# Latent attention with its value products in three reduced-precision passes, and new orders around it

## The reference

```python
h = layer_norm(x) * (1 + sc1) + sh1
proj = h @ w_in[l]                                   # q_c, kv_c, k_r, retention q, k, v, gate
a = mla_mixer(q_c, kv_c, k_r, ...)                   # latent attention, 8 heads
r = retention_mixer(r_q, r_k, r_v, r_g, ...)
y = jnp.concatenate([a, r], axis=-1) @ w_out[l]      # then layer norm, feed-forward, layer norm
# inside mla_mixer, for each head (q, k of 64 plain + 32 rotary columns; v of 64 columns)
sc = q_blk @ k.T * scale                             # masked to the causal half
p = softmax(sc)
out = p @ v
```

## Time and profile before

| | us |
|---|---|
| median of 3 runs | 2687.31 (2684.17 to 2688.14) |
| profiled execution: device time | 2691.6 |
| its span, first to last instruction | 2689.8 |
| PE busy | 2504.4 (93%) |
| DVE, POOL, ACT busy | 1350.4, 733.9, 651.6 |
| mean granted clock of TensorE | 0.963 of full speed |

### The profile page before, as it was taken

How to read it: one execution, slowest core, us unless ns; L and a number is a source line. 1 busy time by engine, 2 the same in 40 slices (tenths; PEclk the granted TensorE clock), 3 DMA queues, 4 the chain that set the end, 5 groups by cost and what they waited for, 6 DMA issues and landing times.

```text
span 2689.8 us, 29003 instructions
## 1 busy us (share of the span) xinstructions
PE 2504.4 (93%) x11544; PEld 1955.2 (73%) x11544; DVE 1350.4 (50%) x1513; ACT 651.6 (24%) x946; POOL 733.9 (27%) x490
## 2 busy tenths in 40 slices
PE   5998779989999999999998689999998999999998
PEld 3776556657678888888886368886586778888877
DVE  7556743434643444444435779996528321314433
ACT  3002224431432001101123421113204200025521
POOL 1241320015463332332345211210045223330011
PEclk9999879999999999999999899999999999979999
DMA  6651000022132332332222121112232521110021
GB/s 225 198 164 61 20 18 8 8 95 86 58 107 83 94 98 75 94 98 87 79 85 79 39 94 41 35 39 102 69 123 82 163 74 47 47 40 1 1 86 71
DMA packets 228851, 206.96 MB, mean 77 GB/s; under 512 B 15248, under 2 KB 203280, under 8 KB 227712
## 3 DMA queue, kind: packets, MB, share of 16 engines
q1 hardware_dynamic: 223552, 178.61, 21.9%
q10 hardware_dynamic: 3840, 21.89, 2.1%
q0 software_dynamic: 1344, 4.91, 0.5%
HBM read 180.35 MB, written 17.83 MB: 74 GB/s over the span
## 4 chain that ended last, share of the span: by engine, by line
PE 78%; DVE 9%; ACT 4%; issue 4%; PEld 2%; POOL 1%; DMA 1%; PEldq 1%; ACTq 0%; DVEq 0%; SPq 0%; POOLq 0%
PE G L1633 28%; PE G L304 25%; PE G L1099 2%; PE M L3001 2%; PE M L307 2%; PE G L2506 1%; PE M L400 1%; PE M L1649 1%; PE G L2322 1%; PE M L2322 1%; PE M L2986 1%; PE M L1010 1%; DVE WMAX L3024 1%; PE G L2349 1%; PE M L2508 1%
## 5 line engine op out<-in xcount | busy, mean ns | idle before, releaser
L278 POOL TENSOR_SCALAR WH<-RAW 128x1024 fp32r<-128x1024 f32 (+1 forms) x154 | 134.2, 872 | 887.2 <-PE G L1633 515.5
L304 PE MATMUL G<-HH,WH 128*128 128x512 f32 x1056 | 336.8, 400 | 14.5 <-POOL WL L2164 7.8
L304 PE MATMUL G<-HH,WL 128*128 128x512 f32 x1056 | 332.5, 396 | 0.0
L304 PE MATMUL G<-HL,WH 128*128 128x512 f32 x1056 | 332.4, 396 | 0.0
L281 POOL TENSOR_TENSOR WL<-RAW,WH 128x1024 fp32r<-128x1024 f32 (+1 forms) x154 | 299.4, 1944 | 12.9
L1633 PE MATMUL G<-HH,WH 128*128 128x512 f32 x640 | 227.2, 404 | 13.3 <-POOL WL L281 8.5
L304 PEld LDWEIGHTS G<-HH,WH 128*128 128x128 f32 x1056 | 188.2, 189 | 61.4 <-issue 19.2
L1633 PE MATMUL G<-HH,WL 128*128 128x512 f32 x640 | 223.8, 398 | 0.0
L1633 PE MATMUL G<-HL,WH 128*128 128x512 f32 x640 | 223.7, 398 | 0.0
L304 PEld LDWEIGHTS G<-HL,WH 128*128 128x128 f32 x1056 | 188.7, 188 | 42.2
L304 PEld LDWEIGHTS G<-HH,WL 128*128 128x128 f32 x1056 | 188.5, 188 | 42.1
(11 more groups left out here) (536 smaller groups left out, 4445.2 us busy)
## 6 DMA issues: line engine op xcount, KB each, us to landing
RAW<-in_w_ff SPq DMA_DIRECT2D x40, 512.0 KB, 3.8
RAW<-in_w_ff SPq DMA_DIRECT2D x80, 256.0 KB, 2.8
WVEC<-in_w_ada SPq DMA_DIRECT2D x24, 512.0 KB, 4.6
FVEC<-in_e_w_mod SPq DMA_DIRECT2D x24, 512.0 KB, 3.8
FVEC<-in_o_w_mod SPq DMA_DIRECT2D x24, 512.0 KB, 3.6
RAW<-in_o_w_in SPq DMA_DIRECT2D x24, 512.0 KB, 3.6
RAW<-in_e_w_in SPq DMA_DIRECT2D x20, 512.0 KB, 3.6
ADA<-in_w_ada SPq DMA_DIRECT2D x4, 2048.0 KB, 19.5
```

Source lines behind the costliest of these rows:

```text
L278: pool.tensor_scalar(hi, raw, 1.0, 0.0, ALU.mult, ALU.add).then_inc(w_high, 1)
L304: m = pe.matmul(G[s][:, n * w:(n + 1) * w], part[s][:, k, :], acts[i][:, k, n * w:(n + 1) * w], start=first, stop=last)
```

## The change

- The value product is split in three float32r passes. ACT still writes the exponentials PF (now three buffers). GpSimd copies them to PH (float32r, two buffers), DVE subtracts to get PL (three buffers), and the values have a high and a low part too (VPH, VPL). `values` now runs two steps behind the loop in place of one.
- In the DVE loop the new subtraction `p_low(g)` stands ahead of `smax(h + 1, i)`.
- The products for the first pair's queries and keys become a lead of mla. The second rotary part moves from head 0 to head 1; `q_part` and `k_part` move to steps 3 and 6, `ROW_AT` to (9, 11) for even heads, `v_part(0)` ahead of the maxima.
- The end of ret is run one head ahead on both engines. The first split of win waits until DVE's chains are done. The wf lead does tiles 4 to 7 of units 0 and 1, then the last `spread`, then tiles 0 to 3 of both; POOL passes the gate ahead of unit 2. In ein POOL makes the high parts of the first four units and not two. In odd three loads change places.

```diff
+        PF, PL = [[at(f"{n}{i}", [P, 512], t, (24 + 2 * i) * kb) for i in range(3)] for n, t in (("PF", F32), ("PL", F32R))]
+        PH = [Z(f"PH{i}", [P, 512], F32R, 12 + 2 * i) for i in range(2)]
...
 # PE, values(g)
-                pe.wait_ge(S("ml_e2"), g + 1)
-                pe.matmul(G[1][:, cols_], VP[:, kb_, first:first + P], PF[g % 4][:, 0:n], start=(kb_ == 0),
-                          stop=(kb_ == 4 * c + 3)).then_inc(S("ml_pv"), 1)
+                pe.wait_ge(S("ml_plo"), g + 1)
+                pe.matmul(G[1][:, cols_], vh, PH[g % 2][:, 0:n], start=(kb_ == 0), stop=False)
+                pe.matmul(G[1][:, cols_], vl, PH[g % 2][:, 0:n], start=False, stop=False)
+                pe.matmul(G[1][:, cols_], vh, PL[g % 3][:, 0:n], start=False, stop=(kb_ == 4 * c + 3))\
+                  .then_inc(S("ml_pv"), 1)
 # PE, the loop
-                if g:
-                    values(g - 1)
+                if g > 1:
+                    values(g - 2)
 # ACT, the exponential of step g
-                need(act, S("ml_pv"), g - 3)
+                need(act, S("ml_pv"), g - 2)
 # DVE
+            def p_low(g):
+                dve.wait_ge(S("ml_ph"), g + 1)
+                dve.tensor_tensor(PL[g % 3][:, 0:n], PF[g % 3][:, 0:n], PH[g % 2][:, 0:n].bitcast(F32), ALU.subtract)\
+                   .then_inc(S("ml_plo"), 1)
...
             for g, (h, c, kb_) in enumerate(STEPS):
+                p_low(g)
                 if i < NT and h + 1 < MLA_HEADS:
                     smax(h + 1, i)
 # POOL
+            for g, (h, c, kb_) in enumerate(STEPS):
+                pool.wait_ge(S("ml_e2"), g + 1)
+                need(pool, S("ml_pv"), g - 1)
+                pool.tensor_scalar(PH[g % 2][:, 0:n], PF[g % 3][:, 0:n], 1.0, 0.0, ALU.mult, ALU.add).then_inc(S("ml_ph"), 1)
 # start and win
+            dve.wait_ge(S("ada_chain"), KT * len(CHAINS))
+            dve.sem_inc(ada_added, 1)
...
+            pool.wait_ge(ada_added, 1)
 # the order of extras in the mla loop (PE)
-                    if i == (1 if h else 4):
+                    if i == 3:
                         q_part(M[1], WQN, j + 1, S("ml_qp"))
-                    if i == (3 if h else 6):
+                    if i == 6:
                         k_part(M[1], j + 1, S("ml_kp"))
-            return (8, 10) if h == 0 else (7, 9)
+            return (7, 9) if h % 2 else (9, 11)
 # wf, POOL and PE's lead
-                if i == 1:
+                if i == 2:
                     gate(pool, current[0])
...
+            for s in range(2):
+                for k in range(4, KT):
+                    products(s, k)
+            spread(pe, N_PAIR - 1)
+            for k in range(4):
+                pe.wait_ge(S("ml_out"), k + 1)
+                for s in range(2):
+                    m = products(s, k)
```

More of the change, by code:

```diff
@@ L439, in start_sp @@
                   .then_inc(S(f"ada{g}"), 16)
+        ada_added = whole("ada_added")
         def start_dve(dve):
@@ L906, in ret_act, with scaled @@
             act.activation(SD[:], MV[:, :, 1], ACT.Sqrt, bias=vec("eps1"), scale=1.0).then_inc(S("ret_sd"), 1)
-            for h in range(RET_HEADS):
+            def scaled(h):
                 act.wait_ge(S("ret_nt"), h + 1)
@@ L912, in ret_act @@
                                scale=vec("gn_g", h)).then_inc(S("ret_t32"), 1)
+            scaled(0)
+            for h in range(RET_HEADS):
+                if h + 1 < RET_HEADS:
+                    scaled(h + 1)
                 act.wait_ge(S("ret_gate"), h + 1)
@@ L995, in passes, with take, mla_products @@
             return ((stationary[0], moving[0]), (stationary[0], moving[1]), (stationary[1], moving[0]))
[L997 to L1003, removed]
+        mla_lead = whole("mla_lead")
+        taken = [0]
+        def take(pe):
+            need(pe, S("ml_free"), taken[0])
+            taken[0] += 1
+        def mla_products(pe):
             def q_part(dst, w, r, signal):
@@ L1012, in q_part, with k_part @@
                 m.then_inc(signal, 1)
-            def k_part(dst, j):
+            def k_part(dst, j, signal):
                 for n in range(2):
@@ L1018, in k_part, with mla_first, spread, mla_pe @@
                         m = pe.matmul(dst[:, 512 * n:512 * n + 512], a, b, start=(i == 0), stop=(i == 2))
-                m.then_inc(S("ml_kp"), 1)
+                m.then_inc(signal, 1)
+            return q_part, k_part
+        def mla_first(pe):
+            q_part, k_part = mla_products(pe)
+            pe.wait_ge(mla_split, N_SPLIT)
+            pe.wait_ge(S("ret_dec"), NT)
+            pe.wait_ge(S("ret_state"), 2 * NT - 2)
+            q_part(G[0], WQN, 0, mla_lead)
+            k_part(G[1], 0, mla_lead)
+        def spread(pe, j):
+            take(pe)
+            if j == 0:
+                pe.wait_ge(moved, info("mla")["dma_end"])
+            pe.wait_ge(S("ml_rec"), 4 * j + 4)
+            for c in range(2):
+                m = pe.matmul(M[1][:, 512 * c:512 * c + 512], SEL[:, c * P:(c + 1) * P], DEN[j % 2][:], start=True,
+                              stop=True)
+            m.then_inc(S("ml_bc"), 1)
+        def mla_pe(pe):
+            q_part, k_part = mla_products(pe)
             def v_part(j):
-                take()
+                take(pe)
                 for t in range(NT):
@@ L1141, in mla_pe @@
             pe.wait_ge(mla_split, N_SPLIT)
-            take()
+            take(pe)
             q_part(M[1], WQR, 0, S("ml_r"))
             q_part(M[0], WQS, 0, S("ml_r"))
-            q_part(G[0], WQN, 0, S("ml_qp"))
-            k_part(G[1], 0)
+            v_part(0)
             pe.wait_ge(S("ml_rot"), 2)
@@ L1161, in mla_pe @@
                 extras(h, i)
-                if g:
-                    values(g - 1)
-            values(len(STEPS) - 1)
-            spread(N_PAIR - 1)
+                if g > 1:
+                    values(g - 2)
+            for g in (2, 1):
+                values(len(STEPS) - g)
         def rope_rows(pe, h, high):
@@ L1638, in wf_lead, with products @@
         def wf_lead(pe):
-            wf_unit(pe, 0)
+            def products(s, k):
+                for part, moving in ((WH, HH), (WH, HL), (WL, HH)):
+                    m = pe.matmul(G[s][:, half(0)], part[s][:, k, :], moving[:, k, half(0)],
+                                  start=(k == 4 and part is WH and moving is HH), stop=(k == 3 and part is WL))
+                return m
+            for s in range(2):
+                pe.wait_ge(w_split[s], wf_U(s) // 2 + 1)
+                need(pe, unit_freed[s], wf_U(s) // 2)
+                if s:
+                    pe.wait_ge(S("ml_num"), 2 * MLA_HEADS)
+                for k in range(4, KT):
[5 more added lines that the diff above has]
+                    m = products(s, k)
+                    if k == 3:
+                        m.then_inc(unit_done[s], 1)
         def norm_mean_pe(pe, tag, h):
```

145 lines of the change are left out of this document (74 added, 71 removed).

## The result

The changed kernel takes 2810.62 us (median of 4 runs, 2809.24 to 2815.32) where the kernel before took 2686.07 on the same chip: ratio 1.0467, 95% interval 1.0448 to 1.0485. The forecast was 2764 and the range 2712 to 2830; the time lies in the range, 47 us above the forecast and within 5 us of the first rival's 2815. In the profiled executions the span went from 2689.8 to 2807.7 us, +117.9 where the sum had +76.5.

The account below looks back on a forecast made before the run. PE was taken as the bound, the ring of maxima just under it. Loop +80, clock +6, way in -10, start -3.5, w_out +4: +76.5 on 2691.6 us, 2768; less 4.3 to the median, 2764; range 2712 to 2830.

Parts of the forecast that it names:

- first rival: Latent attention loop: half clock all through the rings, 0.95 us longer in each of 49; 2815 us in all, chance 0.25.
- The value product: Latent attention loop: three float32r passes cost PE 0.70 us, not 0.88, per 512-column step; about 10 us less over eight heads.
- The ring: Loop steps with a maximum: copy, subtraction, maximum and PE wait in a closed circle; 4.1 us a step, not 2.0.
- second rival: Latent attention loop: the four-engine circle of waits does not close, PE stays the bound; 2649 us, chance 0.08.
- the third (half price): Latent attention loop: maxima partly free of subtractions, or shorter hops, halve the price; +36 us, 2723 us, chance 0.12.
- The clock in the waits: Loop: half clock only after three new 3.6 us waits, 2 us each, +6; full clock taken in the rings.
- prediction's own sign: Granted clock of a bare head's stretch: near 1.00 means the forecast, below 0.8 the first rival.
- The even heads: Heads 2 and 4: a 3.35 us wait goes, the row waits 3.6 us for the keys' low part; +11.6 each.
- Head 7: Last head of the loop, without maxima: PE stays the bound; -1.3 and +1.2 us for the last subtraction, so nothing.
- Start: Kernel's start: DVE's chain without GpSimd beside it ends 4.7 us earlier; -3.5 us in all, ends -5 and -1.
- The way in and w_out: Before the loop: earlier maxima, -10 us (ends -5, -13). After it: unit 2 waits for weights, +4 (ends -3, +6).
- ein: Edits in the ein stage: within 1 us, counted as nothing.

Follow-up runs that it names:

- lows first, filled: Changed kernel with low parts and reciprocals ahead of DVE's subtraction, plus overwritten PE passes (five per step with a maximum, eight at i = 10 of even heads): 2778.21 us.
- filled runs: Changed kernel plus five overwritten PE passes ahead of the scores in steps with a maximum: 2797.85 us; with twenty narrow ones more in even heads: 2790.9 us.
- Lows first: Changed kernel with the low parts of queries, keys and values, and the reciprocals, ahead of DVE's subtraction: 2797.26 us, ratio 1.0403.

## Why the prediction was right in kind and short in size

Where the loop's 133.6 us lie, head by head, from the second scores of a head to those of the next, and for head 7 to the last value product:

| head | 0 | 1 | 2 | 3 | 4 | 5 | 6 | 7 |
|---|---|---|---|---|---|---|---|---|
| predicted | +2.2 | +15.7 | +11.6 | +12.6 | +11.6 | +12.6 | +13.6 | 0 |
| changed kernel | +9.5 | +21.4 | +19.2 | +18.7 | +18.9 | +19.0 | +18.6 | +8.5 |
| lows first, filled | +1.6 | +19.7 | +17.3 | +12.6 | +13.4 | +12.5 | +14.1 | +4.0 |

The prediction has 2 us more for the clock in each of the heads 0, 2 and 4. With these counted in, the heads 0 to 6 were put too low by 5.0 to 6.4 us each, and head 7 by 8.5.

- **The value product.** Right: 0.16 us a step where 0.18 was predicted. In the changed kernel it can be seen only in head 7, where such a step takes 686.61 - 685.25 = 1.36 us; elsewhere PE waits.
- **The ring.** Right in each link and in its sum: 26.6 us at full clock against 27.2 for the rings of head 3, and two independent ways to open it, the order on DVE and a third buffer, each give 89 to 93 us back. The one ring that was worked out, i = 1, was put too high, 4.1 for 3.64: the values of two steps before have 128 columns there and not 512, and the hop from GpSimd to DVE was 0.03 us and not 0.15. i = 5 made up for a part of it (5.38 for 5.1). The second rival (the ring doesn't close) and the third (half price) are refuted by the same rows.
- **The clock in the waits.** This is the step that failed: "They leave PE idle for 2.0 of 4.0 us ... so I take full clock", +6. The busy share of another stretch was the wrong comparison: that one holds four waits of 1.29 to 1.53 us and is over after some 10 us, where the rings go on for seven steps in every head and begin with waits of 2.1 and 1.8 us. Whether it is the length of the waits or their number that brought the clock down, no run here separates. The loop's clock is 0.72, by the prediction's own sign the first rival. The term is at least 19 us by the filled runs. The first rival's mechanism was therefore the right one, but its price, 0.95 us in all 49 rings, was not. In head 3 the granted clock of the seven rings is 1.00, 0.76, 0.50, 0.62, 0.83, 0.63 and 0.76, and in the bare head 6 it is 0.50 in the last five. Yet in head 3 only i = 2, 3 and 5 took longer than at full clock; in the others the slow passes fell where PE would have waited anyway. That the time came so near to the rival's 2815 is luck: what its price had too much was made up by the low parts and head 7, which it left out as my sum did. The Trainium skill ("TensorE: Matmul & The Clock Gate", on oscillation in real kernels) tells of a kernel in which the clock fell anew at every wait. These rows agree in part: the clock fell in every head, but not at every wait, and in heads 1 to 6 it was back at 1.00 in the first ring.
- **The even heads.** I priced the row's wait for the keys' low part at 3.6 us, and it was 3.57. I left out that the product for the keys itself waits 1.7 us for the low part of the queries, since one buffer serves both and q_low stands behind a subtraction; that three steps lay between them looked like enough. Lows first takes 15 us off the loop, 4.6 of it from the row's wait that I had. So the second mis-sized term is some 11 us, with its half clock. It is what DVE's extras cost behind a subtraction, and not the keys' product alone: the edit moved all of them, and head 0 gained most (8.7 us), which I had put at +2.2 and which took +9.5.
- **Head 7.** Predicted without cost; it takes 25.4 in place of 17.0 us. `spread` waits 2.12 us for reciprocals that stand between the subtractions on DVE, then runs at half clock, the scores of a late step wait 1.41 us for an exponential, and the last value product waits 1.1 us for its subtraction. Lows first, which takes the reciprocals out from between the subtractions, gives 3.6 of the 8.5 us back.
- **What stays open.** The loop with both parts taken out is 305.5 us, 97 above before, where rings and extras were priced at 80. By then heads 3, 5 and 6 cost what was predicted for them (last row of the table). The 17 us lie in head 2 (5.7 us above its price), heads 1 and 7 (4.0 each), head 4 (1.8) and 2 us of overwritten passes ahead of the loop's second scores. How much of it is the passes' own cost, what is left of the half clock and the order of the low parts, no run here separates.
- **Start.** Failed: 0 in place of -3.5. The chain went from 8.32 to 3.61 as worked out, but the next long instruction of DVE, T32L, took 3.63 us for two where it took 1.53, beside a part of GpSimd's split that now lies there (L281, 2.34 us from 48.03). The range's end of 1 us gain, by the Trainium skill's rule on the shared port pair ("SBUF — State Buffer"), was the better value; by 220 us nothing was left of even that.
- **The way in and w_out.** -9.8 for a predicted -10. The end of ret gave more than the 3 us that I took: its last instruction on DVE ends at 336.40 in place of 341.81 us. What the lead of mla gave beside it was not tried apart. PE waits 10.56 us for the weights of unit 2, as worked out; the part costs 1.4 us in place of 4.
- **ein.** I put it at nothing, although a wait of 7.8 us stood ahead of it in the trace before. ScalarE's high part of the third unit had to be done before GpSimd's low part; with GpSimd doing both it is 5.0 us less. An edit is only free of effect when the wait in front of it has been looked up.

## What to carry to other kernels

When an engine gets a new short instruction in a loop, ask what stands behind it in that engine's list and whether its input is older: here a maximum that was ready waited behind a subtraction that was not, and three exchanged lines were worth 89 us. A buffer count and a lag that are equal (two copies, values two steps late) leave no moment in which the producer can run ahead. And a wait that comes back in every step can be paid twice on TensorE, once as idle time and once in the clock of what follows: here at least 19 of the loop's 134 us. That another stretch waited for the same share of its time, but in shorter waits and only four of them, said nothing of it.

## What the runs showed of the hardware

- A closed ring with waits of up to 2.1 us (1.4 on average) in steps of mostly 3.5 to 5.2 us brought the granted clock to 0.72 over 342 us. With the waits of head 3 filled to 0.5 to 1.1 us it was 1.00 in all seven rings. A short stretch with 1.43 us of wait in 2.74 had stayed at full speed too.
- Extra work on a waiting engine made the kernel faster: 245 overwritten passes took 11 us off the loop.
- Moving GpSimd's split away from one chain of VectorE put it beside the next instruction: 8.32 to 3.61 us there, 1.53 to 3.63 here.
- Copies of 512 columns cost 0.62 us on GpSimd; the hops were 0.17 us from TensorE to GpSimd, 0.03 from GpSimd to VectorE and 0.05 from VectorE to TensorE, where I had taken 0.15, 0.15 and 0.07.
